# A 64-byte shift of TensorE's moving operands in a two-block transformer kernel on one core

## The reference, cut to what matters

```
x = x + 0.5 * swiglu(rms_norm(x), ffn1_w_in, ffn1_w_out)     # 1024 -> 2 x 2816 -> 1024
x = x + hybrid_mixer(rms_norm(x), ...)   # w_in_mix (xbc, z, q, k, v), SSD scan, diff attention, w_out_mix
x = x + memory_cross_attention(rms_norm(x), rms_norm(mem), w_cq, w_ck, w_cv, w_co)   # mem: 256 tokens
x = x + 0.5 * swiglu(rms_norm(x), ffn2_w_in, ffn2_w_out)
x = rms_norm(x, norm_final_w)
# second block
proj = rms_norm(x) @ w_in;  o = stick_breaking_attention(q, k, v);  y_conv = gated short convolution
x = x + rms_norm((gate_attn * (o @ w_attn_out) + gate_conv * (y_conv @ w_conv_out)) @ w_o)
x = x + rms_norm(square(relu(rms_norm(x) @ w_up)) @ w_down)  # 1024 -> 4096 -> 1024
x = x + sigmoid(rms_norm(x) @ w_ple_gate) * (p @ w_ple_proj)
```

## Time and profile before

| | |
|---|---|
| time, median of 3 runs | 2134.65 us (2134.08 to 2134.89) |
| span of the profiled execution | 2133.4 us |
| PE busy | 2114.8 us, 99% |
| POOL, DVE, ACT busy | 1120.5, 829.8, 803.6 us |
| granted TensorE clock | 1.00 on average |
| DMA | 207.71 MB, 97 GB/s |

### The profile page before, as it was taken

How to read it: one execution, slowest core, us unless ns; L and a number is a source line. 1 busy time by engine, 2 the same in 40 slices (tenths; PEclk the granted TensorE clock), 3 DMA queues, 4 the chain that set the end, 5 groups by cost and what they waited for, 6 DMA issues and landing times.

```text
span 2133.4 us, 29164 instructions
## 1 busy us (share of the span) xinstructions
PE 2114.8 (99%) x10122; PEld 1740.7 (82%) x10122; DVE 829.8 (39%) x1489; ACT 803.6 (38%) x1345; POOL 1120.5 (53%) x1493
## 2 busy tenths in 40 slices
PE   9999999999999999999999999999999999999999
PEld 7888888878887778877888888887787888888887
DVE  5222211762841766143322222208744474023244
ACT  5222232325834655323322223326554343122233
POOL 6555555673354337725655555554545466555554
PEclk9999999999999999999999999999999999999999
DMA  6322233233322213412332223321222223332322
GB/s 214 119 98 98 99 106 106 85 99 96 114 99 79 75 55 122 155 40 89 99 98 98 95 94 117 99 96 63 79 89 79 89 80 108 99 99 99 99 89 80
DMA packets 61344, 207.71 MB, mean 97 GB/s; under 512 B 6616, under 2 KB 8088, under 8 KB 61256
## 3 DMA queue, kind: packets, MB, share of 16 engines
q1 hardware_dynamic: 55216, 195.84, 27.8%
q10 hardware_dynamic: 6040, 10.65, 1.5%
HBM read 204.31 MB, written 4.77 MB: 98 GB/s over the span
## 4 chain that ended last, share of the span: by engine, by line
PE 42%; issue 28%; POOL 27%; DVE 2%; POOLq 0%; ACT 0%; DMA 0%; SPq 0%; DVEq 0%; ACTq 0%
POOL w_lo L463 27%; PE bank L516 11%; PE bank L518 11%; PE bank L517 11%; PE bank L678 1%; PE bank L680 1%; PE bank L679 1%; PE bank L908 1%; PE bank L932 1%; PE bank L840 1%; PE bank L920 0%; DVE gx_lo L2394 0%; DVE bank L2403 0%; PE bank L846 0%; DVE x L2405 0%
## 5 line engine op out<-in xcount | busy, mean ns | idle before, releaser
L463 POOL TENSOR_TENSOR w_lo<-w_raw,w_hi 128x256 fp32r<-128x256 f32 x1448 | 1087.1, 783 | 933.4 <-ACT w_hi L1283 933.3
L516 PE MATMUL bank<-gx_hi,w_hi 128*128 128x512 f32 (+1 forms) x1768 | 674.9, 382 | 7.8 <-DVE gx_lo L2394 4.5
L518 PE MATMUL bank<-gx_hi,w_lo 128*128 128x512 f32 (+1 forms) x1768 | 668.1, 378 | 0.0
L517 PE MATMUL bank<-gx_lo,w_hi 128*128 128x512 f32 (+1 forms) x1768 | 667.6, 378 | 0.0
L1283 ACT CAST w_hi<-w_raw 128x1024 fp32r<-128x1024 f32 x364 | 378.4, 1045 | 347.9 <-PE bank L518 291.8
L516 PEld LDWEIGHTS bank<-gx_hi,w_hi 128*128 128x128 f32 x1768 | 332.6, 188 | 74.2 <-DVE gx_lo L2394 6.4
L518 PEld LDWEIGHTS bank<-gx_hi,w_lo 128*128 128x128 f32 x1768 | 332.5, 188 | 62.1
L517 PEld LDWEIGHTS bank<-gx_lo,w_hi 128*128 128x128 f32 x1768 | 332.7, 188 | 60.5 <-issue 0.2
L516 PE MATMUL bank<-ff_hi,w_hi 128*128 128x512 f32 x352 | 136.9, 389 | 0.0
L517 PE MATMUL bank<-ff_lo,w_hi 128*128 128x512 f32 x352 | 136.9, 389 | 0.0
L518 PE MATMUL bank<-ff_hi,w_lo 128*128 128x512 f32 x352 | 136.9, 389 | 0.0
(11 more groups left out here) (358 smaller groups left out, 2703.4 us busy)
## 6 DMA issues: line engine op xcount, KB each, us to landing
w_raw<-wstream SPq DMA_DIRECT2D x364, 512.0 KB, 3.5
bias_spread<-bias_rows ACTq DMA_DIRECT2D x1, 2560.0 KB
square<-cum_rows ACTq DMA_DIRECT2D x8, 256.0 KB, 3.5
rfin_row<-cum_rows ACTq DMA_DIRECT2D x8, 256.0 KB, 3.1
outT<-ple_o SPq DMA_DIRECT2D x8, 256.0 KB, 2.0
x<-xT SPq DMA_DIRECT2D x3, 512.0 KB, 8.0
square<-bias_spread ACTq DMA_DIRECT2D x4, 256.0 KB, 2.6
rfin_row<-bias_spread ACTq DMA_DIRECT2D x4, 256.0 KB, 2.7
```

The source lines that it names most:

```text
L463: ins = nc.gpsimd.tensor_tensor(w_lo[:, s, part], w_raw[:, s, part], w_hi[:, s, part].bitcast(F32), ALU.subtract)
L516: nc.tensor.matmul(dst, hi, rhs[0], start=first, stop=False)
L517: nc.tensor.matmul(dst, hi, rhs[1], start=False, stop=False)
L518: return nc.tensor.matmul(dst, lo, rhs[0], start=False, stop=last)
```

## The change

The change adds 64 bytes to the start of every moving activation of the rounded products. `gx_hi` and `gx_lo` begin at a multiple of 2048 plus 64, and the cursor is brought back to a multiple of 2048 behind them, so that `w_raw`, `w_hi` and `w_lo` begin at such multiples as before. In the region `ff`, `ys`, `o`, `ox`, `cv`, `o2`, `up` and `p` get a `shift` of 64. So that a shifted tensor does not run into its neighbour, `at` adds 512 bytes for each full 8 KB of `kb`; `m_hi` and `m_lo` keep their 64 bytes. `p_lo` moves to 12.25 KB as well, and so begins 320 bytes behind a multiple of 512. Room for this comes from the DMA scratch, which shrinks from 16384 to 1024 bytes.

`prob`, `w_T`, `o_nrm` and the other tensors of `in_gx` move with `gx` by 64 bytes. `gx` is also the stationary operand of `token_group` in `z`, `v` and `v2`. No instruction is added, removed or moved; on every engine the order and the waits are the same.

```diff
+GAP = 512
+SHIFT = {"gx": 64, "ff": 64, "ys": 64, "o": 64, "ox": 64, "cv": 64, "o2": 64, "up": 64, "p": 64}
...
-        cursor[0] = -(-cursor[0] // LINE) * LINE
+        cursor[0] = -(-cursor[0] // LINE) * LINE + SHIFT["gx"]
         GX_HI, GX_LO = cursor[0], cursor[0] + DC * S * 4
         gx_hi = fixed("gx_hi", [DC, S], F32R)
         gx_lo = fixed("gx_lo", [DC, S], F32R)
+        cursor[0] = -(-cursor[0] // LINE) * LINE
         w_raw = fixed("w_raw", [RING, UNIT])
...
-        REGION = -(-cursor[0] // 512) * 512
-        cursor[0] = REGION + 96 * 1024 + 64
+        REGION = -(-cursor[0] // LINE) * LINE
+        cursor[0] = REGION + 96 * 1024 + 12 * GAP + 512
...
-        def at(name, kb, shape, dt=F32):
-            off = REGION + int(kb * 1024)
+        def at(name, kb, shape, dt=F32, shift=0):
+            off = REGION + int(kb * 1024) + int(kb // 8) * GAP + shift
...
-        ff_hi = at("ff_hi", 0, [FC, S], F32R)
-        ff_lo = at("ff_lo", 44, [FC, S], F32R)
+        ff_hi = at("ff_hi", 0, [FC, S], F32R, shift=SHIFT["ff"])
+        ff_lo = at("ff_lo", 44, [FC, S], F32R, shift=SHIFT["ff"])
...
-        p_hi = at("p_hi", 8, [2, S], F32R)
-        p_lo = at("p_lo", 12, [2, S], F32R)
-        ple_t = at("ple_t", 16, [2, S])
-        ple_g = at("ple_g", 20, [2, S])
+        p_hi = at("p_hi", 8, [2, S], F32R, shift=SHIFT["p"])
+        p_lo = at("p_lo", 12.25, [2, S], F32R, shift=SHIFT["p"])
+        ple_t = at("ple_t", 16.25, [2, S])
+        ple_g = at("ple_g", 20.25, [2, S])
...
-    nc = bacc.Bacc("TRN2", target_bir_lowering=False, num_devices=1)
+    nc = bacc.Bacc("TRN2", target_bir_lowering=False, num_devices=1, dynamic_dma_scratch_size=1024)
```

More of the change, by code:

```diff
@@ L257, in build @@
         ysq_tmp = at("ysq_tmp", 69, [GH * SHD])
-        ys_hi = at("ys_hi", 16, [DC, S], F32R)
-        ys_lo = at("ys_lo", 32, [DC, S], F32R)
+        ys_hi = at("ys_hi", 16, [DC, S], F32R, shift=SHIFT["ys"])
+        ys_lo = at("ys_lo", 32, [DC, S], F32R, shift=SHIFT["ys"])
         q_T = at("q_T", 48, [AH, S])
@@ L307, in build @@
         bias_h = [square, rfin_row]
-        o_hi = at("o_hi", 48, [AH, S], F32R)
-        o_lo = at("o_lo", 64, [AH, S], F32R)
+        o_hi = at("o_hi", 48, [AH, S], F32R, shift=SHIFT["o"])
+        o_lo = at("o_lo", 64, [AH, S], F32R, shift=SHIFT["o"])
         load_sq = at("load_sq", 0, [DC, S])
@@ L324, in build @@
         qx_T = at("qx_T", 48, [DC, S])
-        ox_hi = at("ox_hi", 64, [DC, S], F32R)
-        ox_lo = at("ox_lo", 80, [DC, S], F32R)
+        ox_hi = at("ox_hi", 64, [DC, S], F32R, shift=SHIFT["ox"])
+        ox_lo = at("ox_lo", 80, [DC, S], F32R, shift=SHIFT["ox"])
         m_sum = at("m_sum", 40.0625, [ML])
@@ L333, in build @@
         v2_tok = at("v2_tok", 16, [TT, S])
-        cv_hi = at("cv_hi", 24, [4, S], F32R)
-        cv_lo = at("cv_lo", 32, [4, S], F32R)
+        cv_hi = at("cv_hi", 24, [4, S], F32R, shift=SHIFT["cv"])
+        cv_lo = at("cv_lo", 32, [4, S], F32R, shift=SHIFT["cv"])
         gates = at("gates", 40, [16, S])
-        o2_hi = at("o2_hi", 0, [4, S], F32R)
-        o2_lo = at("o2_lo", 8, [4, S], F32R)
+        o2_hi = at("o2_hi", 0, [4, S], F32R, shift=SHIFT["o2"])
+        o2_lo = at("o2_lo", 8, [4, S], F32R, shift=SHIFT["o2"])
         cc_t = at("cc_t", 64, [S])
@@ L366, in build @@
         post_sum = rfin_row
-        up_hi = at("up_hi", 16, [HC, S], F32R)
-        up_lo = at("up_lo", 48, [HC, S], F32R)
+        up_hi = at("up_hi", 16, [HC, S], F32R, shift=SHIFT["up"])
+        up_lo = at("up_lo", 48, [HC, S], F32R, shift=SHIFT["up"])
         f_acc = at("f_acc", 80, [DC, S])
```

## The result

The changed kernel takes 2150.68 us (median, 2150.34 to 2151.26) where the kernel before takes 2134.77 us beside it: ratio 1.0074, 95% interval 1.0059 to 1.0088. It is slower by 15.9 us. The forecast was 2120.2 us, and its range ended at 2142. The span of the profiled execution grew from 2133.4 to 2149.5 us, by 16.1.

What follows compares the result with a forecast made beforehand. PE was taken as the bound, its time the sum of distances between matmul starts. Terms of -15.9, -1.7 and +3.2 us gave -14.4 against the 2133.4 us span, plus 1.25 for the median: 2120.2 us, range 2110 to 2130 (8 in 10: 2070 to 2142).

Steps and rivals of the forecast that it cites:

- Term 1: Products with weights stationary, 512 columns, moving operand from 0 to 64: 7344 gain 2.17 ns each, -15.9 us.
- Term 2: Products with weights stationary, 256 columns, moving operand from 0 to 64: 768 gain 2.17 ns each, -1.7 us.
- Term 3: Products with activations (`gx`) stationary at 64, weights moving at 0: 480 lose 6.67 ns each, +3.2 us.
- Terms 4 to 6: Plain float32 matmuls: zero, 2 us either side; `p_lo`, `m`, `wdt`: under 0.2 us each; scratch, gaps, shifted writes: nothing.
- B: Rival: 512-column products at 64 miss a 6.667 ns grid step, 233.33 ns each, 49 us lost, 2185 us; chance 0.15.

Runs made afterwards that it cites:

- The maps: Three kernels of only matmul stretches on PE, nothing of the reference, varying operand places and columns; 512 columns: 226.67 ns at equal 0, 228.9 at 64/0 (moving/stationary).
- third map: PE-only matmul stretches, nothing of the reference, varying places and what ran before: 256 columns at 448 took 113.3 ns behind 512 or 384 columns, 117.8 behind 192.

## Why the prediction was wrong

**What bounds the kernel: right.** PE's distances alone moved the end. No other engine or wait came up.

**Term 1: the step that failed.** It priced the 7344 products of 512 columns by the nearest row, `m` with 256 columns, with the words "the fixed part was independent of the columns at address 0, so I carry its 13.33 - 11.16 = 2.17 ns over: -15.9 us". The independence was read at address 0 and used at address 64. The maps show that at 64 what is left beyond the columns is 11.1 ns at 256, 13.3 at 320 to 448, and 15.5 at 512. So each product lost 2.2 ns where 2.17 were to be gained. At address 0 the two sizes compared happened to agree: others leave from 11.6 ns (288 columns) to about 16.5 (464 and 480). And the 117.83 ns of the row carried over is one of two steady states of that place (113.3 is the other, in the run with every shift 256), so it was not a price of the place alone. Over the 7344 products the distances grew by 14.4 us, a little less than 7344 x 2.2 = 16.2. The 6783 of them that were between 224 and 230 ns before grew by 2.3 each, 15.6 us; the 559 that were longer already fell by 1.1 us in sum.

**Term 2: right in kind.** 120.0 ns became 117.8; in sum 1.0 us was gained instead of 1.7.

**Term 3: right.** +2.6 us for +3.2. The row it was read from, `m` stationary, had the case itself and not a neighbour of it.

**Terms 4 to 6: right.** The other matmuls moved by 0.3 us. `m`, which was to stay, gained 0.3: 17 of its 192 distances with `m` moving were 113 or 114 ns after the change, none before. The layout and the scratch cost nothing measurable (ratio 1.0000).

**The rivals.** B had the right side and the right products, but it took all of them to 233.33 ns and so 2185 us.
## What to carry to other kernels

A price per matmul holds for its own number of columns and its own pair of places; before it is carried to another shape, a stretch of 48 matmuls of that very shape is the nearest measurement, and one such kernel maps fifty cases. At 512 columns these maps foretold the kernel (228.9 and 233.3 ns in both). At 256 columns they did not always, since there the same places had two steady states. For fp32r products with 512 moving columns and 128 weight columns, start the moving and the stationary operand at the same place modulo 256 bytes, both at multiples of 32. Plain alignment of both to 256 or more does that. At 256 columns other places are shorter, so a shift that helps one stage can cost another.

## What the runs showed of the hardware that was not expected

- At 512 columns and 128 weight columns the distance between fp32r matmuls depends on the operands' places modulo 256 bytes: 226.67 ns when they agree (at 0, 32, 64, 128, 256 or 448 each), 228.9 with moving at 64 and stationary at 0, up to 240.0 ns.
- At 256 columns it is the reverse: 120.0 ns when they agree, 113.3 to about 120 elsewhere.
- At 128 and 192 columns it is 111.6 to 111.8 ns at the three places tried.
- With both operands at 0, loading 16 or 32 weight columns instead of 128 made the distance at 512 moving columns longer (228.9 and 231.6 ns).
- With 256 columns the same stretch can run steadily at 113.3 or at 117.8 ns. In the third map what ran before it decided which, and in the kernel `m` at 64 shows both.
